# Two-layer hybrid backbone on one core: a bank wait moved to the fifth token tile, a square sum moved, down and out tiles 0 and 1 interleaved, bank pairs begun anew per layer

## The reference, cut to what matters

```
h  = modulate(rms_norm(x, norm1), sh1, sc1)              # latent and context, own modulation
z  = h @ w_in                                            # columns split among four branches and gate logits
a, b, c, d = retention(z), gated_linear(z), gqa(z), differential(z)
m  = sum_i sigmoid(gates_i) * (branch_i @ w_branch[i])
x  = x + g1 * (m @ w_out)
h2 = modulate(rms_norm(x, norm2), sh2, sc2)
u  = h2 @ w_up
x  = x + g2 * ((silu(conv3(u[:2816])) * u[2816:]) @ w_down)
```

## Time and profile before

| | |
|---|---|
| median of three runs | 2664.07 us |
| profiled execution, own time | 2669.89 us |
| its span, first to last instruction | 2668.1 us |
| PE busy | 2551.5 us, 96% |
| POOL busy | 1489.9 us, 56% |
| DVE busy | 1343.7 us, 50% |
| ACT busy | 760.8 us, 29% |
| mean granted clock of TensorE | 0.985 |

### The profile page before, as it was taken

One profiled execution on the slowest core, in us unless ns is written; L12 is line 12 of the kernel. 1 busy time (PEld: TensorE's weight loads), 2 busy tenths in 40 slices (PEclk: granted clock), 3 DMA queues, 4 the chain that ended last, 5 costly groups with the idle time before them and its releaser, 6 DMA issues.

```text
span 2668.1 us, 37757 instructions
## 1 busy us (share of the span) xinstructions
PE 2551.5 (96%) x15408; PEld 2119.6 (79%) x15408; DVE 1343.7 (50%) x1807; ACT 760.8 (29%) x1276; POOL 1489.9 (56%) x1375
## 2 busy tenths in 40 slices
PE   5999999999999999999999999999998999999999
PEld 2788888877777888888878888797877778888777
DVE  3622256543577776555564562327654677511231
ACT  4611333432355521111120132133522454111200
POOL 3443468523424627666669336448834445688886
PEclk9999999999999999999999999999998999999999
DMA  7422422313213734444434462122311246433322
GB/s 272 150 74 91 116 58 70 91 54 94 76 42 121 256 106 127 123 116 125 120 99 123 122 213 78 57 55 73 82 57 48 71 126 218 119 95 96 96 83 81
DMA packets 378209, 285.09 MB, mean 107 GB/s; under 512 B 10309, under 2 KB 338729, under 8 KB 377526
## 3 DMA queue, kind: packets, MB, share of 16 engines
q1 hardware_dynamic: 375744, 279.81, 35.0%
q10 hardware_dynamic: 1686, 2.78, 0.3%
q0 software_dynamic: 608, 0.09, 0.0%
HBM read 253.28 MB, written 29.36 MB: 106 GB/s over the span
## 4 chain that ended last, share of the span: by engine, by line
PE 79%; DVE 9%; POOL 4%; ACT 3%; issue 2%; DMA 2%; ACTq 0%; DVEq 0%; SPq 0%; POOLq 0%
PE ps L533 18%; PE ps L534 17%; PE ps L535 17%; PE ps L1204 3%; PE ps L739 3%; PE ps L577 2%; PE ps L578 2%; PE ps L579 2%; POOL w_lo L1358 2%; PE ps L823 2%; DVE ffl L2487 2%; PE ps L843 2%; PE ps L1153 1%; POOL w_hi L1355 1%; PE ps L770 1%
## 5 line engine op out<-in xcount | busy, mean ns | idle before, releaser
L1355 POOL TENSOR_TENSOR w_hi<-ring,tiny 128x512 fp32r<-128x512 f32 x480 | 535.4, 1116 | 984.6 <-PE ps L535 574.4
L533 PE MATMUL ps<-hh,w_hi 128*128 128x512 f32 (+1 forms) x2320 | 841.8, 363 | 10.8 <-DVE hl L2040 9.9
L1358 POOL TENSOR_TENSOR w_lo<-ring,w_hi 128x512 fp32r<-128x512 f32 (+1 forms) x568 | 801.4, 1413 | 81.0 <-ACT w_hi L1561 43.2
L534 PE MATMUL ps<-hl,w_hi 128*128 128x512 f32 (+1 forms) x2320 | 819.9, 353 | 0.0
L535 PE MATMUL ps<-hh,w_lo 128*128 128x512 f32 (+1 forms) x2320 | 818.9, 353 | 0.0
L533 PEld LDWEIGHTS ps<-hh,w_hi 128*128 128x128 f32 x2320 | 442.8, 191 | 103.0 <-issue 27.7
L535 PEld LDWEIGHTS ps<-hh,w_lo 128*128 128x128 f32 x2320 | 441.7, 190 | 61.6
L534 PEld LDWEIGHTS ps<-hl,w_hi 128*128 128x128 f32 x2320 | 442.8, 191 | 56.5 <-issue 1.0
L1680 ACT ACTIVATE arena<-ps,tiny,vec 128x768 f32<-128x768 f32 (+1 forms) x120 | 108.7, 906 | 187.3 <-DVE tiny L2217 187.2
L1852 ACT ACTIVATE arena<-ps,vec 128x768 f32<-128x768 f32 (+1 forms) x44 | 39.0, 888 | 424.8 <-PE ps L535 424.8
L2496 DVE SCALAR_TENSOR_TENSOR arena<-ps,vec,arena 128x511 f32<-128x511 f32 x66 | 43.6, 660 | 219.9 <-ACT arena L1852 219.1
(11 more groups left out here) (270 smaller groups left out, 3797.6 us busy)
## 6 DMA issues: line engine op xcount, KB each, us to landing
ring<-in_w_in SPq DMA_DIRECT2D x118, 512.0 KB, 4.0
ring<-in_w_mod SPq DMA_DIRECT2D x96, 512.0 KB, 3.9
ring<-in_w_up SPq DMA_DIRECT2D x88, 512.0 KB, 4.2
ring<-in_w_down SPq DMA_DIRECT2D x48, 512.0 KB, 3.6
ring<-in_w_out SPq DMA_DIRECT2D x32, 512.0 KB, 3.7
logits<-arena SPq DMA_DIRECT2D x32, 384.0 KB, 2.6
arena<-logits SPq DMA_DIRECT2D x32, 384.0 KB, 4.3
ring<-in_w_down SPq DMA_DIRECT2D x24, 384.0 KB, 3.2
```

The costliest lines, as they stand in the source:

```text
L533: pe.matmul(acc, wh[:, offset + k], hi[:, n, x:y], start=n == 0, stop=False)
L534: pe.matmul(acc, wh[:, offset + k], lo[:, n, x:y], start=False, stop=False)
L1355: pool.tensor_tensor(wh[:, 0:count], w, one[:].unsqueeze(2).to_broadcast([P, count, P]), ALU.mult).then_inc(*up("w_lead", ("lead", key, j)))
L1358: pool.tensor_tensor(wl[:, 0:count], w, wh[:, 0:count].bitcast(F32), ALU.subtract).then_inc(*up("w_split", ("split", key, j)))
```

## The change

Five edits. (1) `token_part` asks only for the first two banks at the start, and for the third bank's old holder ahead of the group that first writes it (`t * wide == 1024`, the fifth); where four groups do (layer 1's second pairs) the third bank isn't taken. (2) `turn` is set to 0 at each layer's start. (3) `out` tiles 0 and 1 are made half by half in turns. (4) Layer 1's second square sum goes behind `up` tile 0's first part, as in layer 0. (5) `down` tiles 0 and 1 go half by half in turns over their three chunks each, and chunk order and POOL's split order follow.

```diff
--- before.py
+++ after.py
@@ -226,8 +226,9 @@
         slices = next_modulation(l)
         for c in range(2 * FT):
                 order += [("up", l, c)] + (slices[c - 1:c] if c > 0 else [])
-        for n in range(3 * KT):
-            order += [("down", l, n // 3, n % 3)] + (slices[2 * FT + n // 3 - 3:2 * FT + n // 3 - 2] if n % 3 == 0 and n >= 6 else [])
+        order += [("down", l, u, c) for c in range(3) for u in range(2)]
+        for n in range(6, 3 * KT):
+            order += [("down", l, n // 3, n % 3)] + (slices[2 * FT + n // 3 - 3:2 * FT + n // 3 - 2] if n % 3 == 0 else [])
         order += [("dctx", l, n // 3, n % 3) for n in range(3 * KT) if W[l] > LAT]
     return order
 
@@ -507,7 +508,7 @@
 
         @block.tensor
         def _(pe):
-            tenant, used, turn = {}, [0], [0]
+            tenant, used, turn, in_third = {}, [0], [0], [None]
 
             def room(key, *banks):
 
@@ -563,12 +564,18 @@
                     for key in keys:
                         next_chunk(key)
                     first = 3 if pair[0] >= 2 else 0
-                    for s, n in room(("tt", l, b, pair[0]), first, first + 1, first + 2):
+                    third = tenant.get(first + 2)
+                    for s, n in room(("tt", l, b, pair[0]), first, first + 1):
                         pe.wait_ge(s, n)
+                    if len(pair) * tiles > 8:
+                        tenant[first + 2] = ("tt", l, b, pair[0])
+                        in_third[0] = third
                 if t == 0:
                     for key in keys:
                         pe.wait_ge(*at(("split", key, j)))
                 wide = len(pair) * P
+                if j == 0 and t * wide == 1024 and in_third[0]:
+                    pe.wait_ge(*at(("free", in_third[0])))
                 wh, wl = (w_pair(w, keys, j) for w in (w_hi, w_lo))
                 ts, to = slice(t * P, (t + 1) * P), psum(("tt", l, b, pair[0]), 1536)[:, t * wide:(t + 1) * wide]
                 bank_begins, bank_ends = t * wide % 512 == 0, (t + 1) * wide % 512 == 0 or t == tiles - 1
@@ -1048,6 +1055,8 @@
                 def behind(b, slot):
                     for key in slices_behind(l, b, slot):
                         modulation_slices(key)
+
+                turn[0] = 0
 
                 def banks():
                     turn[0] += 1
@@ -1141,8 +1150,18 @@
                                 mm = pe.matmul(acc[:, x:y], wl[:, wk], hh[:, n, x:y], start=False, stop=k == 1)
                         mm.then_inc(*up("pe_half", ("full", acc_key), *([("half", key, b // 2)] if b % 2 else [])))
                 (x, y), (y, z) = (PARTS[l, 2][part] for part in ("first", "second"))
-                for u in range(KT):
-                    projection(("out", l, u), mh, ml, y, (u % 4,), each=(lambda k: ("ml", l, 0, k)) if u == 0 else None)
+                pair = [("out", l, 0), ("out", l, 1)]
+                for n, key in enumerate(pair):
+                    next_chunk(key)
+                    for s, c in room(key, n):
+                        pe.wait_ge(s, c)
+                for j, key in itertools.product(range(2), pair):
+                    pe.wait_ge(*at(("split", key, j)))
+                    product(psum(key)[:, 0:y], key, j, mh, ml, 0, y, first=KT // 2 * j,
+                            each=(lambda k: ("ml", l, 0, k)) if key == pair[0] else None).then_inc(
+                        *up("pe_half", ("half", key, j), *([("full", key)] if j else [])))
+                for u in range(2, KT):
+                    projection(("out", l, u), mh, ml, y, (u % 4,))
                 for u in range(KT):
                     key = ("oraw", l, u)
                     next_chunk(key)
@@ -1156,7 +1175,7 @@
                         sum_of_squares(l, 2, "first")
                 pair = [("up", l, 0), ("up", l, 1)]
                 for n, key in enumerate(pair):
-                    if n == (1 if W[l] > LAT else 0):
+                    if n == 1:
                         sum_of_squares(l, 2, "second")
                     next_chunk(key)
                     for s, c in room(key, 2 * n, 2 * n + 1):
@@ -1177,7 +1196,20 @@
                         sum_of_modulation(l + 1, c // KT - 1, 2 * ((c + 3) % 4), 2 * ((c + 3) % 4) + 1)
                     if l + 1 < DEPTH and c % KT == 1 and c > KT:
                         sums_turned(l + 1, c // KT - 1)
-                for u in range(KT):
+                for u in range(2):
+                    for s, n in room(("down", l, u), u):
+                        pe.wait_ge(s, n)
+                for c in range(3):
+                    for u in range(2):
+                        next_chunk(("down", l, u, c))
+                    count = min(8, FT - 8 * c)
+                    for j, u in itertools.product(range(2), range(2)):
+                        key = ("down", l, u, c)
+                        pe.wait_ge(*at(("split", key, j)))
+                        mm = product(psum(("down", l, u))[:, 0:LAT], key, j, ffh, ffl, 0, LAT, count=min(4, count - 4 * j),
+                                     first=8 * c + 4 * j, whole=FT, each=(lambda k: ("ffl", l, k)) if u == 0 else None)
+                        mm.then_inc(*up("pe_half", ("half", key, j), *([("full", ("down", l, u))] if 2 * c + j == 5 else [])))
+                for u in range(2, KT):
                     acc_key = ("down", l, u)
                     for s, n in room(acc_key, u % 4):
                         pe.wait_ge(s, n)
@@ -1189,7 +1221,7 @@
                         for j in range(2):
                             pe.wait_ge(*at(("split", key, j)))
                             mm = product(acc[:, 0:LAT], key, j, ffh, ffl, 0, LAT, count=min(4, count - 4 * j),
-                                         first=8 * c + 4 * j, whole=FT, each=(lambda k: ("ffl", l, k)) if u == 0 else None)
+                                         first=8 * c + 4 * j, whole=FT)
                             mm.then_inc(*up("pe_half", ("half", key, j), *([("full", acc_key)] if 2 * c + j == 5 else [])))
                 if l + 1 < DEPTH:
                     for u in range(KT):
@@ -1364,6 +1396,8 @@
                 while done[0] < end:
                     first = split_chunks[done[0]]
                     pair = next(p for p in token_pairs(first[2]) if first[3] in p) if first[0] == "t" else (0,)
+                    if first[0] == "down" and first[2] < 2:
+                        pair = (0, 1)
                     split(*split_chunks[done[0]:done[0] + len(pair)])
                     done[0] += len(pair)
```

## The result

The changed kernel took 2650.24 us (median of 6 runs, 2647.75 to 2651.96), the kernel before 2663.61 beside it (6 runs, 2662.58 to 2669.72). The two medians are 13.4 us apart. The forecast time was 2645, the measured one is 2650.24, inside the range. The profiled execution took 2650.26 us, 19.6 less than the one of before. Those of before scatter more, and the one profiled was at their slow end.

A forecast was written before the change was run, and what follows sets the result against it. TensorE (PE), busy 96% of the span, was taken as the bound, so only its waits and slow clock could pay. Terms 2.8 + 7.4 - 0.2 + 7 + 1.0 + 0.8 = 18.8 us; 2664.07 - 18.8 = 2645, range 2631 to 2657.

The forecast's parts named there:

- (a): Layer 0's first retention token tile: 3.38 us wait for ACT becomes 1.9 for POOL, half the dip goes; 2.8 us.
- (b): Layer 1, banks reset: token tile's 4.0 us wait, 2.7 dip and first feature's 0.69 wait go; 7.4 us, 0.2 lost at transposes.
- (c): Down tiles 0 and 1 interleaved: each pair falls from 39.55 to 36 us at POOL's pace; 7 us in all.
- nothing lost: Down pairs: a ring slot comes free 3.2 us later, but the next chunk is wanted two rounds on; no cost.
- (d): Layer 1's out tiles 0 and 1: PE waits 2.7 us for POOL, both tiles end about 1 us earlier; 1.0 us.
- The gap stays long, and the dip with it: Layer 1's out tiles: PE's wait remains long, so the clock dip behind it remains too.
- (e): Layer 1's second square sum: 2.85 us wait filled, a new 1.5 us wait before the second parts; 0.8 us.
- Full gain in (c): Rival: in the down pairs POOL keeps ahead and rests stay near their mean; 30 us, 2634; chance 0.13.
- Half lost: Rival: dips stay, down pairs give 3 us for 7, out tiles and square sum nothing; 9 us, 2655; chance 0.17.
- The change doesn't do what it says: Rival: POOL is late at layer 1's token tile too and takes all in the down pairs; 2658; chance 0.09.
- The slower one: Rival: the reset makes four more places in layer 1 wait for ACT's drain, 26.4 us against 19.2 won; 2671; chance 0.03.

The follow-up runs named there:

- e1: The kernel before with the third-bank wait alone (edit to `token_part`); 0.9992 of the kernel before's time, 2.1 us faster [-0.8, 5.1].
- e7: The changed kernel with down tiles 0 and 1 interleaved in layer 1 only; 0.9946 of the kernel before's time.
- e12: The changed kernel, ACT making high parts of chunks 0, 1 in layer 0's down tiles 2 to 7 and chunks 1, 2 in layer 1's pair; 2643.5 us, 0.9900.
- e2: The kernel before with the reset of `turn` per layer alone; 0.9989 of its time, 2.9 us faster [0.5, 5.6].
- e4: The kernel before with down tiles 0 and 1 interleaved alone, both layers; 0.9964 of its time, 9.6 us faster [6.1, 13.1].
- e3: The kernel before with the third-bank wait and the reset of `turn` together; 0.9956 of its time, 11.7 us faster [7.5, 16.0].
- e9: The changed kernel, ACT making high parts in layer 0's down tiles 2 to 7 (chunks 0, 1) and both layers' down pairs (chunks 1, 2); 2652.18 us, 0.9938.
- e8: The changed kernel with ACT making the high parts of chunks 0 and 1 in layer 0's down tiles 2 to 7; 0.9925 of the kernel before's time.
- e5: The kernel before with out tiles 0 and 1 interleaved alone; 0.9993 of its time, 1.9 us faster [-0.5, 4.3].
- e6: The kernel before with layer 1's second square sum moved behind the first wide part alone; 1.0002 of its time, 0.5 us slower [-1.9, 3.2].
- e11: The changed kernel timed again, with nothing altered; 0.9930 of the kernel before's time, 18.7 us faster [15.5, 21.9].
- e10: The changed kernel with ACT making layer 1's high part of out chunk 1 ahead of the last four sigmoids; 0.9933 of the kernel before's time.

## Why the prediction was right, point by point

**(a) Right: 2.6 us for 2.8.** The wait for POOL that was to be late next is there, 1.90 us to the predicted 1.9. The dip shrank by 1.15 us (1.3 taken). In e1, e7 and e12 it went wholly, which is the upper bound of 4.2. The step of 0.114 us per matmul is a little low: two of the 51 matmuls counted in 5.8 us were under way when the window began, and starts in the rows lie 0.12 us apart. No term moves by more than 0.1 us or so for it.

**(b) Right.** The wait 4.20, the dip 2.69, the first feature 0.93 for 0.69: 7.8 us for 7.4. The feature's term was low because the wait counts from the modelled end of a matmul, while its successor could have started earlier. The dip was taken from one execution; e2's and e4's traces have it at 1.6, so some 6.7 is the usual worth. The reset's price: 0.20 us at the transposes, as foretold. That only both edits together do this was an argument in the prediction and is shown by e1 to e3.

**(c) 5.5 us for 7, and here a step failed.** The pair was right: POOL's pace, 36 us forecast and 35.5 and 34.7 measured, with 3.5 us per layer forecast and 3.76 and 4.23 measured. That POOL sets it is borne out in layer 1 by e9 and e12, where half of its work on two chunks went to ACT and the pair fell by another 2.6 us. What failed is the step "nothing lost" behind it. I looked at ring slots, and did not ask for POOL's lead: it leaves the pair without one, and in layer 0 its work per tile (15.8 us beside DVE's modulation steps) is more than PE's 14.95. The clue lay in the trace of before, which has two waits for w_lo in its later down tiles. It cost 2.5 us (e4, e7), and e8 gave it back.

**(d) 1.0 forecast, open.** That PE would wait 2.7 us for w_lo at tile 1 was right (2.44). "The gap stays long, and the dip with it" was right in e5 alone. What the term left out is that PE starts again before the last `ml` is there: at 2217.49, 1.9 us ahead of its end at 2218.85 + 0.56 = 2219.41, where it used to start behind it. Tile 2's first matmul, before and after:

```profile
2238.72 0.31 PE L533 MATMUL ps<-mh,w_hi 128*128 128x256 f32 x1
...
2223.28 0.28 PE L534 MATMUL ps<-mh,w_hi 128*128 128x256 f32 x1
```

It starts 6.0 us behind the last `ml`'s end before and 3.9 after. In the kernel before all 27 matmuls that were left ran 0.21 us apart (half clock), in the changed kernel 14 of the 36. But the kernels with the old order scatter by as much: 3.4 us in e3, 4.9 in e4 and e6, 5.5 and 5.8 in e2 and e1. With the new order it is 4.0 in e7, e9, e11 and e12, 5.0 in e5 and 5.7 in e8. The means, 5.1 and 4.4 us (e10 left out), are 0.7 us apart, with a scatter of about 1 us in each group. So a gain near the forecast 1.0 is possible, and neither the traces nor e5's time tell it from 0.

**(e) 0 for 0.8.** I had one new wait of 1.5 us; there are two, 1.07 and 1.66, one per second part. Where no dip falls into the ledger's last row it is 19.3 to 19.5 us long with the edit and without it. The dip behind the waits, 1.3 to 1.5 us, is there in six of eight traces with this edit and in two of six without, too few to put a price on it.

**The sum and the arrival.** With the terms measured, 2.6 + 7.8 - 0.2 + 5.5 = 15.7 us, where the ratio says 15.7 [12.8, 18.4] and, the second time, 18.7 [15.5, 21.9]. Nothing between the stretches took it back: in the profiled executions the time from the first matmul to the last fell by 18.9 us, these 15.7, 1.5 at the out tiles and 1.7 elsewhere, where dips differ. The agreement to the tenth is luck: an execution carries several us of dips that come and go, and with (b) at its usual worth the sum is 14.6. Not luck are (a), (b) and the pairs of (c), each forecast to within 0.8 us with the mechanism named. The forecast was 3 us too high for two reasons: the 2.5 us lost behind layer 0's pair, and the 1.8 us of (d) and (e), which no run shows.

**The clock.** By the traces the dips of (a) and (b) stand behind their waits: with the wait in layer 1 gone the clock there is 1.00 in all eight traces of kernels that have both edits (27 or 36 matmuls start in 5.8 us in the six without, 49 in the eight with). The Trainium skill, "TensorE: Matmul & The Clock Gate", section "HAM oscillation", is borne out where the wait is long (4 us). Where it is 0.5 to 3 us, the same wait is followed by a dip in one execution and not in the next.

**The rivals.** Full gain in (c) failed because POOL did not idle but worked for 31.9 of 35.5 us. "Half lost" had the right reason in part: something taken back behind the pair. "The change doesn't do what it says" is excluded by the traces: layer 1's token tile waits for nothing, so POOL was not late there, and (c)'s pairs are 3.76 and 4.23 us shorter. The slower one is excluded by e2; its sum took 19.2 us as won where the terms above it make 19.0, which changes nothing.

## What to carry to other kernels

When a helper engine feeds the bound one through a short ring, ask not only whether it keeps pace in the stretch that is sped up but with what lead it leaves it, and compare its work per tile with the bound engine's over the tiles behind: two thirds of a pair's gain were lost again over the tiles behind it. Test two edits that share a resource together as well as alone: a moved wait and a changed bank gave 2 to 3 us each (the first within its noise), both together 12. And where single executions scatter by several us in dips, compare the traces between the same instructions: most waits repeat to 0.2 us, where the times of five rounds leave an interval of 3 us either way. A gain that hangs on a dip needs several traces of each order, as (d) shows.

## What the runs showed of the hardware

VectorE's subtraction of two SBUF operands (128x512) takes 0.68 us alone, and GpSimd's two steps of a split 1.04 and 1.29 us. Beside each other each takes about 1.5 to 1.8 us, and in e9's layer 1 their starts alternate, one of VectorE's and one of GpSimd's every 1.70 us: they take turns. An unbroken row of VectorE's can also keep GpSimd out wholly, 7.69 us for one instruction while twelve rests ran at 0.6 us each (e9). The Trainium skill, "SBUF — State Buffer", section "Who interferes with whom", has the port pair that the two engines share as an exclusive lock, and VectorE instructions with two SBUF inputs as contending for it with GpSimd's reads. Turns agree with a lock. A lock that is given up after each instruction would have had GpSimd wait for one rest and not for eleven, as measured; what kept it out is open.

The dip behind a wait of given length isn't a constant: behind 4 us in layer 1 it cost 2.7 us in two traces and 1.6 in four. Behind the out tiles' 3.0 us all matmuls left ran at half clock in one trace and hardly any in another (27 of 27 in before, 1 of 27 in e3), and behind shorter waits it cost 0 or about 1.5 us.
